# The second layer's output projection as seven block products per 2x2 block, with the weight split shared out anew

## The reference, cut to what matters

```python
merged = sigmoid(gl_m) * (y_m @ w_out_m) + sigmoid(gl_g) * (y_g @ w_out_g)
x = x + gate[:, None] * (merged @ w_out)     # the out projection, 1024 x 1024
...
y = x * rsqrt(mean(x * x) + EPS) * final_norm_w   # once, after layer 1
```

## Time and profile before

| | |
|---|---|
| device time, 3 runs | 1440.89 us median (1440.36 to 1442.1) |
| span of the profiled execution | 1438.0 us |
| TensorE busy, by the page | 99% |
| VectorE / ScalarE / GpSimd busy | 68% / 33% / 71% |
| mean granted TensorE clock | 0.998 |

### The profile page before, as it was taken

One profiled execution on the slowest core, in us unless ns is written; L12 is line 12 of the kernel. 1 busy time (PEld: TensorE's weight loads), 2 busy tenths in 40 slices (PEclk: granted clock), 3 DMA queues, 4 the chain that ended last, 5 costly groups with the idle time before them and its releaser, 6 DMA issues.

```text
span 1438.0 us, 27064 instructions
## 1 busy us (share of the span) xinstructions
PE 1422.0 (99%) x10191; PEld 1382.6 (96%) x10191; DVE 983.8 (68%) x1454; ACT 474.4 (33%) x1086; POOL 1027.1 (71%) x1421
## 2 busy tenths in 40 slices
PE   8999999999999999999999999999999999999997
PEld 5999998999999999999999999989999999999997
DVE  5865566674777679889978676567566876868234
ACT  4332223313766423101243323241257661320122
POOL 1688875596655489998859897558765556979772
PEclk9999999999999999999999999999999999999999
DMA  9222333123566465444332242411346665453222
GB/s 359 60 64 75 130 108 121 56 70 110 150 189 192 144 262 197 144 164 145 113 133 74 79 128 87 137 60 59 103 127 182 170 189 187 159 188 120 74 74 89
DMA packets 113838, 189.54 MB, mean 132 GB/s; under 512 B 12736, under 2 KB 76352, under 8 KB 112320
## 3 DMA queue, kind: packets, MB, share of 16 engines
q1 hardware_dynamic: 42736, 138.34, 28.8%
q10 hardware_dynamic: 70992, 49.63, 11.7%
HBM read 169.79 MB, written 18.15 MB: 131 GB/s over the span
## 4 chain that ended last, share of the span: by engine, by line
PE 96%; DVE 2%; DMA 0%; ACT 0%; issue 0%; DVEq 0%; SPq 0%; ACTq 0%
PE acc L603 78%; PE acc L570 6%; PE X L843 2%; PE X L808 2%; PE X L570 1%; PE X L828 1%; PE X L875 1%; PE X L854 1%; PE X L762 1%; DVE cv L1631 1%; PE acc L721 0%; DVE ssq L1432 0%; DMA xr<-in_xT 0%; DVE h_pre L1484 0%; DVE xr L1949 0%; PE X L815 0%
## 5 line engine op out<-in xcount | busy, mean ns | idle before, releaser
L513 POOL CAST w_hi<-w_st 128x256 fp32r<-128x256 f32 x704 | 419.3, 609 | 388.7 <-issue 187.3
L517 POOL TENSOR_TENSOR w_lo<-w_st,w_hi 128x256 fp32r<-128x256 f32 x704 | 645.8, 927 | 0.0
L603 PE MATMUL acc<-h_hi,w_hi 128*128 128x320 f32 x1744 | 406.2, 314 | 0.8 <-ACT h_hi L1049 0.8
L603 PE MATMUL acc<-h_lo,w_hi 128*128 128x320 f32 x1744 | 397.8, 309 | 1.5 <-DVE h_lo L1478 1.5
L603 PE MATMUL acc<-h_hi,w_lo 128*128 128x320 f32 x1744 | 397.4, 309 | 0.0
L603 PEld LDWEIGHTS acc<-h_hi,w_hi 128*128 128x128 f32 x1744 | 288.6, 188 | 10.6 <-issue 7.5
L603 PEld LDWEIGHTS acc<-h_lo,w_hi 128*128 128x128 f32 x1744 | 291.5, 188 | 2.2 <-DVE h_lo L1478 2.0
L603 PEld LDWEIGHTS acc<-h_hi,w_lo 128*128 128x128 f32 x1744 | 291.5, 188 | 0.0
L1631 DVE SCALAR_TENSOR_TENSOR cv<-raw,convw_sb,cv 128x642 f32<-128x642 f32 x128 | 134.9, 1054 | 4.5
L1391 DVE SCALAR_TENSOR_TENSOR ada_acc<-ada_st,sc,ada_acc 128x512 f32<-128x512 f32 x112 | 107.1, 995 | 1.8
L1145 ACT ACTIVATE cvt<-cv 128x642 f32<-128x642 f32 x32 | 23.8, 743 | 158.1 <-DVE cv L1631 158.1
(11 more groups left out here) (257 smaller groups left out, 2468.4 us busy)
## 6 DMA issues: line engine op xcount, KB each, us to landing
w_st<-in_wts SPq DMA_DIRECT2D x176, 512.0 KB, 3.6
cum_bc<-cum_dram ACTq DMA_DIRECT2D x80, 256.0 KB, 5.0
ada_st<-in_wada SPq DMA_DIRECT2D x33, 512.0 KB, 4.4
ex_bc<-ex_dram ACTq DMA_DIRECT2D x64, 128.0 KB, 3.2
ada_pre<-in_wada SPq DMA_DIRECT2D x15, 512.0 KB, 10.0
mga_dram<-c_buf SPq DMA_DIRECT2D x16, 320.0 KB, 6.0
xf<-xf_dram SPq DMA_DIRECT2D x4, 1280.0 KB, 7.2
mga<-mga_dram SPq DMA_DIRECT2D x2, 2560.0 KB, 9.9
```

The source lines that it names most:

```text
L513: nc.gpsimd.tensor_copy(quarter(w_hi, slot, q), quarter(w_st, slot, q)).then_inc(s_pool, 1)
L517: nc.gpsimd.tensor_tensor(quarter(w_lo, slot, q), quarter(w_st, slot, q), f(quarter(w_hi, slot, q)), ALU.subtract).then_inc(w_split, 1)
L603: last = mm(a[:, hf, 0:n1], w[:, s, cols], x[:, k, hf * HALF:hf * HALF + n1], start=(k == 0 and n == 0), stop=(k == KC - 1 and n == 2))
```

## The change

The out projection of layer 1 (8 output tiles, 8 input chunks, 640 tokens) is cut into four units q of two output tiles. For each, the input channels are halved (4 chunks each) and the tokens are halved (320 each), and the four blocks of the result come from seven products of 4 chunks x 3 = 12 matmuls of 320 columns, instead of eight. With weight blocks w(tile, input half) and token blocks of the merged activations, the products m = 1..7 use w(0,0), w(0,1), the sum w(1,0)+w(1,1) (m=5), that minus w(0,0) (m=6), w(0,0)-w(1,0) (m=7), w(0,1) minus the m=6 one (m=3) and w(1,1) (m=4); the activations are `b11`, `t1`, `b2`, `t23`, `t4` (blocks and their differences), each with a hi and a lo part.

- VectorE makes the sums of activations and of weights (`add_weights`, four of 128x512 a unit), puts the products together (`read`: additions of products in `m_sums`, and additions to `xr`), and still sums the squares.
- ScalarE casts the weight blocks (`unit_hi`, 28 of 128x512) into a ring of 8, and copies product 1 (`m1_copy`); GpSimd only subtracts (28 of 128x512, `ulo_ready`). Before, GpSimd did both for these tiles.
- TensorE runs 28 products over six PSUM banks; product n waits for its weight unit's lo part and for the bank of product n-6.
- Weights of the odd units go to a second staging area, `w_odd`; the load for q=1 waits for all plain tiles, for q=2 and 3 for the last lo part of unit q-2.
- In `T_M` of layer 1 the `glm` tiles run four ahead of the `om` tiles: glm 0 to 3, then om and glm in turn, and the last four tiles are om 4 to 7. Four gate buffers instead of two.
- The final norm's two parts are the token halves, second half first; its sums stand ahead of the last product, its broadcast within it.

```diff
+        for u in range(NPR):
+            pool.wait_ge(uhi_ready, u + 1)
+            nc.gpsimd.tensor_tensor(ring(1, u), unit_source(u), f(ring(0, u)), ALU.subtract).then_inc(ulo_ready, 1)
...
+        def product(n, hooks=()):
+            q, m = PRODUCTS[n]
+            u = UNITS.index((q, m))
+            if n >= BANKS:
+                bank_freed(pe, n - BANKS)
+            else:
+                evacuated(pe, N_PLAIN - 2 + n // 4)
...
+            pe.wait_ge(ulo_ready, u + 1)
+            for i in range(KH):
+                if q == 0 and m not in (7, 3):
+                    pe.wait_ge(mix_lo, mix_count(m, i))
+                for k, (w, x) in enumerate(((0, hi), (1, hi), (0, lo))):
+                    last = mm(product_bank(n), ring(w, u)[:, P * i:P * (i + 1)], x[:, i, cols],
+                              start=(i == 0 and k == 0), stop=(i == KH - 1 and k == 2))
...
+PRODUCTS = ([(0, m) for m in (1, 5, 2, 6)] + [(1, 1)] + [(0, m) for m in (7, 3, 4)] + [(1, m) for m in (5, 6, 2, 7, 3, 4)]
+            + [(2, m) for m in (1, 5, 6, 2, 7, 3, 4)] + [(3, m) for m in (1, 5, 6, 3, 7, 2, 4)])
+UNITS = [(0, m) for m in (1, 2, 5, 6, 7)] + [(1, 1)] + [(0, m) for m in (3, 4)] + PRODUCTS[8:]
...
+                for i in range(KH - 1):
+                    merge(KH + i, scaled[KH + i])
+                    differences(i)
+                    second_half_low(i)
+                    differences_low(i)
+                add_weights(0)
+                add_weights(1)
+                merge(KC - 1, scaled[KC - 1])
+                add_weights(2)
+                second_half_low(KH - 1)
...
+                read(0)
+                differences(KH - 1)
+                read(1)
+                differences_low(KH - 1)
+                add_weights(3)
+                late = [(n + 1, "read", n) for n in range(2, NPR)]
+                late += [(2.5, "t4", 0), (3.5, "t4lo", 0)]
+                late += [(u - 4.6, "sum", SUMS.index((q, SUM_OF[m]))) for u, (q, m) in enumerate(UNITS) if q > 0 and m in SUM_OF]
+                late += [(TILE_AT[j] + 2.5, "square", j) for j in range(6)]
...
+                for u in (0, 1, 2):
+                    unit_hi(u)
+                second_half_hi(KH - 1)
+                unit_hi(3)
+                differences_hi(KH - 1)
+                warm_root()
+                late = [(0.1, "unit", 4), (1.1, "unit", 5), (2.1, "unit", 6), (2.2, "unit", 7), (2.3, "t4", 0)]
+                late += [(PRODUCTS.index((q, 1)) + 1, "m1", q) for q in range(4)]
+                late += [(u - 4.4, "unit", u) for u in range(RING, NPR)]
+                late += [(TILE_AT[j] + 1.7, "square", j) for j in range(6)]
...
+        for n in range(NPR - 1):
+            product(n)
+        last_sums(0, False)
+        product(NPR - 1, [(2, lambda: last_bc(0))])
+        last_sums(1, False)
+        last_sums(1, True)
+        last_bc(1)
```

More of the change, by code:

```diff
@@ L205, in build @@
     ACTB = KC * TOK * 4
-    h_hi = new("h_hi", [P, KC, TOK], F32R)
+    r_hh = region(ACTB)
+    h_hi = place("h_hi", [P, KC, TOK], r_hh, F32R)
     r_hl = region(ACTB)
@@ L301, in build @@
     rv = new("rv", [P, NCH, 1])
-    rst = new("rst", [P, 2, NCH])
+    rst = new("rst", [P, 2, 6])
     eps_sb = new("eps_sb", [P, 1])
@@ L449, in _ @@
         load_consts()
-        for t in range(2, DEPTH * NT):
+        for t in range(2, N_PLAIN):
             L, p = divmod(t, NT)
@@ new lines, in last_sums @@
+        def last_sums(part, tile7):
+            if tile7:
+                pe.wait_ge(lsq_ready, 4)
+            else:
+                pe.wait_ge(ssq_ready, 2 * DEPTH + 1 + part)
+            for c, row in enumerate(LAST_ROWS[part]):
+                src = c_buf[1] if tile7 else ssq
+                last = mm(X[0][:, 4 * part + c:4 * part + c + 1], src[:, row:row + P], ones[:, 0:1],
+                          start=(part == 0 or (c == 0 and not tile7)), stop=(part == 0 or (c == 2 and tile7)))
+            if part == 0 or tile7:
+                last.then_inc(stat_ready, 1)
@@ L1315, in _ @@
+            for j in range(8):
+                gate_tanh(j)
                 if j == 0:
@@ new lines, in _, with add_out @@
+            x_parts = {}
+            def add_out(q, e, half, src, done=None):
+                for v, c0, c1 in ((0, 0, CTX), (1, CTX, HALF)) if half == 0 else ((1, 0, HALF),):
+                    cols = slice(half * HALF + c0, half * HALF + c1)
+                    last = STT(out=xr[:, 2 * q + e, cols], in0=src[:, c0:c1], scalar=mods[:, 3 * L + 2, v, 2 * q + e:2 * q + e + 1],
+                               in1=xr[:, 2 * q + e, cols], op0=ALU.mult, op1=ALU.add)
+                if done is None:
+                    x_parts[q, e, half] = own.mark(last)
+                else:
+                    last.then_inc(done, 1)
@@ new lines, in add_last, with last_rstd @@
+            def add_last(k, half):
+                rows = slice(half * HALF, half * HALF + HALF)
+                dve.wait_ge(lsq_ready, 2 * (1 - half) + k + 1)
+                ins = TT(ssq[:, rows], ssq[:, rows], c_buf[k][:, rows], ALU.add)
+                if half == 1 and k == 0:
+                    own.link(ins)
+                else:
+                    ins.then_inc(ssq_ready, 1)
+            def last_rstd(part):
+                dve.wait_ge(root_ready, 2 * DEPTH + 1 + part)
+                nc.vector.reciprocal(rst[:, 1, 3 * part:3 * part + 3], rst[:, 0, 3 * part:3 * part + 3]).then_inc(rstd_ready, 1)
@@ L1889, in _ @@
+            for j in range(8):
+                p = T_M + 2 * j
+                later(p)
+                merge(j, gate_scale(j))
                 if p in JOB_AT[L]:
```

480 lines of the change are left out of this document (350 added, 130 removed).

## The result

The changed kernel takes 1451.65 us (median of 4 runs, 1451.45 to 1451.99) against 1440.68 us for the kernel before, timed beside it: a ratio of 1.0076, interval 1.0064 to 1.0088. So it is slower by 11 us, 9 us more than forecast and 3 us beyond the range. The profiled execution took 1451.99 us, its span is 1450.3 us, 12.3 more than before. (The time grew by 11.0 and the span by 12.3, as the median lay 2.9 us above the span before and lies 1.4 above it now.)

The account below looks back on a forecast made before the run. TensorE, busy for 99% of the span, was taken to bound the kernel. -7.1 + 5.1 + 2.4 + 0 + 1.1 = +1.5 us gave span 1439.5; with 2.9 us outside it, 1442.4 us, 8-in-10 range 1436.5 to 1448.5.

Parts of the forecast that it names:

- Part 1: Out projection matmuls on TensorE: 384 become 336, 1.77 us per product; -7.1 us if nothing waits.
- Part 2: ScalarE's casts, copy, squares and weights in the out projection: 7.9 of 12.4 us per unit, hidden.
- Part 3: GpSimd's 28 subtractions of 512 columns: a turn of 1.2 us, alone 8.8 of 12.4 us per unit, hidden.
- Part 6: `T_M` with its tiles in another order: costed at 0, 1 us if the cover were gone.
- Part 7: After the last matmul: +1.1 us (0.5 to 2); the first part's norm inside the last product: 0.
- Part 5: Entry to the products: TensorE stands from t = 15.1 to 19.3 before product 4; +5.1 us, least +2.6, at most 6.
- the turns: At the SBUF, VectorE instructions with two SBUF inputs and GpSimd's instructions alternate, each waiting for the other's to end.
- Part 4: VectorE in the out projection: 10.4 us work plus 3.2 waits, 13.6 per unit against 12.4; +2.4 us, 0 to 4.5.
- Rival D: Slower: VectorE waits a full GpSimd turn in most pairs; +9 instead of +2.4, 1446 to 1451 us, chance 0.13.
- rival E: Slower: TensorE's clock falls behind the 4 us entry stop, 4 to 5 us more; 1446 to 1447 us, chance 0.10.

Follow-up runs that it names:

- e_glm_only: The kernel before with only the new order of `glm` and `om` tiles in layer 1 and four gate buffers; 1440.11 us, ratio 0.9999.
- e_zero_lo: Changed kernel with GpSimd writing zeros, reading nothing, in place of its 28 subtractions; part of the computation left out; 1435.76 us, ratio 0.9967.
- e_nosums: Changed kernel without the twelve weight sums of the second to fourth unit, plain weight blocks in their place; 1441.23 us, ratio 1.0005.
- e_psum_table_halves: e_psum_table with GpSimd's subtractions in two pieces of 256 columns from the ninth weight unit on; 1442.28 us, ratio 1.0014.
- e_nosums_filler8: e_nosums with eight unneeded matmuls on TensorE ahead of product 4; 1439.19 us, ratio 0.9993.
- e_all_filler6: e_psum_table_halves with six unneeded matmuls on TensorE ahead of product 4; 1441.98 us, ratio 1.0012.
- e_table: Changed kernel with ScalarE's table load for the root behind the last gate tanh, not ahead of unit 4's cast; 1451.52 us, ratio 1.0072.
- e_psum_table: e_table with VectorE's partial sum `t` in a free PSUM bank for the first three units; 1449.24 us, ratio 1.0064.

## Why the prediction was wrong

**What held.** Part 1: products that don't wait start every 1.76 us. Part 2: ScalarE was busy for at most 5.02 us of 7.00 in the out projection. Part 3: GpSimd's subtraction took 1.28 us at the least, 1.52 on average. Part 6: 0, by e_glm_only. Part 7's tail: +1.1, measured +1.1. Part 5's order: unit 5's lo part was worked out to t = 19.3; TensorE started on it at 1381.13, which is 19.4 when product 0, at 1368.81, is t = 7.1. This is no luck: unit 4's cast, the copy, unit 5's cast and unit 4's lo part ended within 0.3 us of the forecast too. The mechanism of the turns was right as well; e_zero_lo shows it by taking one side away. It is also what the Trainium skill states (SBUF — State Buffer, "Who interferes with whom": such a pair fully blocks), and the runs agree, 1540 ns against 680.

**The step that failed is in Part 7: "The first part's norm inside the last product costs TensorE about 2 us, as it did inside the last tile (...): 0".** In the kernel before, VectorE had 4.6 us of 7 to spare, so its sum of squares was there when TensorE asked. In the changed kernel VectorE is in arrears. Its timeline at the end:

```profile
1427.42 0.55 DVE L2164 SCALAR_TENSOR_TENSOR xr<-acc,mods,xr 128x320 f32<-128x320 f32 x1
1427.89 0.48 DVE L2174 TENSOR_TENSOR m_sums<-acc,m_sums 128x320 f32<-128x320 f32 x1
...
1431.31 0.49 DVE L2174 TENSOR_TENSOR m_sums<-acc,m_sums 128x320 f32<-128x320 f32 x1
...
1432.93 0.49 DVE L2209 TENSOR_TENSOR ssq<-ssq,c_buf 128x320 f32<-128x320 f32 x1 [0.54 <-ACT c_buf L1490]
```

Product 25 ended at 1427.03 and VectorE reads it at 1431.31 (the third row), 4.3 us later; the last sum of squares, which the column sums want, begins at 1432.93. The lead of several products lets TensorE run ahead, and hides VectorE's lag only until something needs all of VectorE's work. That is the norm ahead of the last product: +6.4 where the forecast had 0, some 5 of it the longer pause and 1.3 the lower clock behind it. The forecast had even "spared" the second half of the last unit, because no sums are left there: it asked when the lag reaches TensorE by way of the weights and forgot the other way, by way of the results. e_nosums (pause 0.51 us, same entry) and e_psum_table_halves (last product 1.5 us behind the one before) both take it away by taking VectorE's waits away.

**The term that was mis-sized: Part 4, VectorE's waits.** Forecast 13.6 us per unit of seven, 3.2 of it waits. VectorE reads the same product (m = 6) of the second, third and fourth unit at

```profile
1397.41 0.50 DVE m_sums L2174
...
1412.23 0.49 DVE m_sums L2174
```

(from the chain that ended last) and at 1427.89 (above): 14.8 and 15.7 us. Beside the same instructions of e_zero_lo, 4.3 and 5.7 us of these are waits at the SBUF; 0.7 us of the first is idle time for ScalarE, and the work itself is 9.8 and 10.0, near the forecast's 10.4. The middle came to +5.0, against a charge of +2.4 and a bound of 4.5. The rest was carried to the end: these three products had ended 3.7, 5.1 and 5.6 us before VectorE read them, so most of the lag was there by product 9, out of the entry and the first unit.

The twelve later weight sums took 1.29 us on average, close to the 1.2 of the forecast: four at 0.68, without a wait, and five at 1.76 to 1.78, which wait out 1.1 us of GpSimd's 1.3. The product 12 x 0.6 x 0.7 = 5 was thus right, and its discount to 3.2, because "VectorE's PSUM work often covers the turn", was wrong. One reading, not tested, is that the engine that has waited goes next, so that a backlog on both sides makes them meet nearly every time. Rival D, from 5 us of waits per unit, is nearest, and its sign, sums at 1.7 us, is seen in five of twelve; its 1446 to 1451 is still short of 1451.65, as it spared the last unit's half too.

**Part 5 by size, and rival E.** +7.2 against +5.1. The pause was as forecast; the rest is nearly all rival E's clock: products 4 and 5 took 3.3 and 2.15 us to the next start instead of 1.77, 1.9 us together. The sum had no term for it, though E's sign, a clock at its lower level behind the first gap, came as written. Its price at the entry is 2.0 to 2.6 us with the sums left out (e_nosums against e_nosums_filler8), and was 0 where the weight units behind were late anyway (e_all_filler6). For the changed kernel itself no run took the fall away. That TensorE is not on the chain between 1362 and 1405, and that e_table started product 4 by 1.8 us earlier and gained 0.1, both speak for nearly none. The 1.3 us of the last product are another matter: there its matmuls are on the chain.

**Small slips.** The sum added 2.9 us for what lies outside the span; for the changed kernel the median lies 1.4 above it, which hid 1.5 us of the miss: the span was missed by 10.8 us, the time by 9.2. The least of Part 5, with product 4 at 16.4, is a product 8 at 23.5 and +2.2, not 23.9 and +2.6; 4608 columns at 0.55 us for 512 are 4.95 us and not 4.8. None of them changes the outcome.

## What to carry to other kernels

Before trading matmuls for additions, add up not only the busy time of VectorE and GpSimd but also their waits for each other's turns at the SBUF. Here half a turn of GpSimd's, times the share of time in which it holds the SBUF, for each VectorE instruction with two SBUF inputs came out right without a discount: 5 us per unit, measured 4.3 and 5.7. A pool of buffers hides a lag only as long as nothing needs the lagging engine to be level: look for that place (a norm, a barrier, the tail) and charge the whole of the arrears there. When an earlier start comes to nothing, find the next unit in the queue before crediting it: here 1.8 us of table load and 2 us of clock were both measured, and both swallowed while VectorE and GpSimd were behind.

## What the runs showed of the hardware

- The length of GpSimd's instruction decides who waits. At 512 columns VectorE's sum takes up to 1.78 us and GpSimd's weight unit 1.3 to 1.5; at 4 x 128, 0.8 to 0.95 and 2.3 to 2.4; both engines' waits add to 28 us either way. At 2 x 256 from the ninth weight unit on, on top of e_psum_table, GpSimd filled its time and the kernel gained 7 us. The four pieces were cut from the first weight unit on and without `t` in PSUM, so the two cuts are not compared like with like.
- Moving one of two inputs to PSUM took an addition's wait away entirely (1000 to 408 ns for 192 columns), and the sum of squares, with two SBUF inputs, went from 1196 to 1720 ns.
- A pause of 3.8 us without a matmul was followed by the lower of TensorE's two clock levels: matmuls every 0.267 us, 16 in a row (1381.13 to 1385.27), and then the upper level again. The 4.5 us without a matmul ahead of the column sums were followed by the lower level too (0.58 in 1432 to 1439). In e_nosums, whose first pause is alike, eight plain float32 matmuls of 256 columns in it kept the clock at 1.00.
- A shorter pause went both ways: with 2.5 us from the last matmul's start to product 4's, product 4 took 3.2 us in e_psum_table_halves (clock 0.76 in 1376 to 1383) and 1.8 in e_psum_table (1.00), where the clock fell behind the next pause (0.88 in 1383 to 1390).
- A plain float32 matmul of 256 columns takes 0.38 us, one of 320 columns in fp32r 0.147, both at a clock of 1.00.
